# A fused two-block transformer step on Trainium2: the delta rule's inverse by six doubling levels of 64-column products, the gate's silu in two gaps, and a shorter router shift

## The reference, cut to what matters

```python
def gated_delta_rule(q, k, v, g, beta):          # 4 heads, chunks of the sequence
    ...
    a_low = jnp.where(strict, einsum('bnhie,bnhje->bnhij', kb, kc) * decay, 0.0)
    lhs = a_low + jnp.eye(C)
    u = triangular_solve(lhs, vb, left_side=True, lower=True)
    w = triangular_solve(lhs, kb * exp(gc)[..., None], left_side=True, lower=True)
    ...                                          # then the scan over chunks: state, outputs
# in hybrid_mixer
    o = rms_norm(o, dn_norm_w) * silu(dz)        # the gate's silu
    return concatenate([attn_out, dn_out], -1) @ w_out
# in routed_moe, with h = norm(x) * (1 + scale2) + shift2
    logits = xt @ w_router + b_router
```

## Time and profile before

| | |
|---|---|
| median of 3 runs | 2151.72 us (2151.05 to 2152.26) |
| the profiled execution | 2151.87 us, its span 2150.0 us |
| mean granted TensorE clock | 0.994 |
| PE busy | 2079.7 us (97%) |
| PE weight load | 1149.2 us (53%) |
| DVE busy | 978.7 us (46%) |
| ACT busy | 327.8 us (15%) |
| POOL busy | 50.3 us (2%) |
| chain that ended last | PE 80%, DMA 12%, DVE 4% |
| HBM | 590.91 MB read, 276 GB/s over the span |

### The profile page before, as it was taken

The page is one execution under the profiler, slowest core; times in us unless marked ns, Lnnn a source line. Parts: engine busy times, 40 slices in busy tenths (PEclk is TensorE's granted clock), DMA queues, the critical chain, the costliest instruction groups (busy, mean ns, idle before and its releaser), DMA issues.

```text
span 2150.0 us, 24181 instructions
## 1 busy us (share of the span) xinstructions
PE 2079.7 (97%) x9736; PEld 1149.2 (53%) x9736; DVE 978.7 (46%) x1573; ACT 327.8 (15%) x730; POOL 50.3 (2%) x30
## 2 busy tenths in 40 slices
PE   5999999999999999999999899999999999999999
PEld 3858533333333333333233456878884648868874
DVE  1486443333333333333322255734676167626684
ACT  1142100000010000000000113311110113311110
POOL 0001000000000000000000002000000011000000
PEclk9999999999999999999999999999999999999999
DMA  9548199999999999999999735324442634244441
GB/s 372 215 190 359 61 383 414 428 428 428 428 428 426 427 428 428 427 427 428 428 427 427 290 136 179 139 85 158 149 157 98 223 119 158 103 132 150 149 157 53
DMA packets 132917, 593.53 MB, mean 276 GB/s; under 512 B 9247, under 2 KB 65743, under 8 KB 104651
## 3 DMA queue, kind: packets, MB, share of 16 engines
q1 hardware_dynamic: 132810, 592.01, 69.4%
HBM read 590.91 MB, written 3.18 MB: 276 GB/s over the span
## 4 chain that ended last, share of the span: by engine, by line
PE 80%; DMA 12%; DVE 4%; issue 1%; ACT 1%; POOL 0%; SPq 0%; POOLq 0%; DVEq 0%
PE bank L1620 23%; PE bank L676 21%; DMA ring<-in_w_dram 11%; PE bank L686 8%; PE bank L2749 6%; PE bank L2712 3%; PE bank L1761 2%; PE bank L2727 2%; PE bank L1601 2%; PE bank L955 2%; PE bank L3103 1%; PE bank L1637 1%; DMA ring<-in_w_ada_dram 1%; DVE arena L1285 1%; PE bank L590 1%
## 5 line engine op out<-in xcount | busy, mean ns | idle before, releaser
L1620 PE MATMUL bank<-ring,arena 128*64 128x512 f32 x2304 | 509.8, 594 | 12.6 <-DMA ring<-in_w_dram 11.1
L676 PE MATMUL bank<-wide,ring 128*128 128x256 f32 x2368 | 517.2, 381 | 2.8 <-ACT wide L2980 2.6
L676 PEld LDWEIGHTS bank<-wide,ring 128*128 128x128 f32 x2368 | 451.0, 191 | 67.5 <-issue 5.9
L1620 PEld LDWEIGHTS bank<-ring,arena 128*64 128x64 f32 x2304 | 161.0, 137 | 351.3 <-issue 321.5
L1261 DVE TENSOR_SCALAR arena<-bank 128x512 f32<-128x512 f32 x32 | 22.1, 692 | 377.2 <-PE bank L1620 377.2
L686 PE MATMUL bank<-ring,wide 128*128 128x512 f32 (+2 forms) x384 | 151.4, 554 | 0.0
L2409 DVE SCALAR_TENSOR_TENSOR arena<-bank,arena 128x254 f32<-128x254 f32 (+1 forms) x176 | 76.6, 476 | 84.7 <-ACT arena L2553 83.2
L686 PEld LDWEIGHTS bank<-ring,wide 128*128 128x128 f32 x384 | 72.6, 190 | 74.6 <-issue 71.3
L1265 DVE RECIPROCAL arena<-arena 128x512 f32<-128x512 f32 x32 | 107.3, 3353 | 1.1
L1437 ACT ACTIVATE arena<-arena 128x512 f32<-128x512 f32 x32 | 20.1, 629 | 493.9 <-DVE arena L1261 493.9
L1620 PE MATMUL bank<-wide,arena 128*64 128x512 f32 x392 | 89.0, 595 | 0.7 <-ACT arena L1441 0.7
(11 more groups left out here) (515 smaller groups left out, 1961.4 us busy)
## 6 DMA issues: line engine op xcount, KB each, us to landing
ring<-in_w_dram SPq DMA_DIRECT2D x144, 2048.0 KB, 25.7
wide<-in_w_dram SPq DMA_DIRECT2D x24, 2048.0 KB, 26.3
arena<-in_w_dram SPq DMA_DIRECT2D x22, 2048.0 KB, 28.4
ring<-in_w_up_dram SPq DMA_DIRECT2D x44, 1024.0 KB, 6.8
ring<-in_w_in_dram SPq DMA_DIRECT2D x21, 2048.0 KB, 8.3
ring<-in_w_ada_dram SPq DMA_DIRECT2D x12, 2048.0 KB, 9.2
ring<-in_w_down_dram SPq DMA_DIRECT2D x10, 2048.0 KB, 7.8
ring<-in_w_out_dram SPq DMA_DIRECT2D x6, 2048.0 KB, 9.3
```

What stands on the lines that cost most here:

```text
L676: ins = pe.matmul(B.bank(name, j)[:, i * T:(i + 1) * T], w[:, k, (first + i) * P:(first + i + 1) * P], hT[:, k, :], start=(k == 0), stop=( ...
L1620: ins = pe.matmul(bank[g * SLOTS:(g + 1) * SLOTS, :], lhsT, rhs[:, g * CH:(g + 1) * CH], start=start, stop=stop)
```

## The change

The squares (`p2`, `p4`, `zz`, `xx`) go. The inverse starts from blocks of 2 (the identity minus the pairs' lower elements, masks `pair` and `pairT`) and doubles in six levels, 2 to 128. In a level a product takes only the columns that change: every second group of columns of the right operand, 64 of 128, so a job is four products of 64 columns (still eight instructions) into half a bank, its copy and its update handle half the elements. `T1` gets a zeroed place per level (GpSimd memsets), `BT` two places. The scaled operands are made before the levels. The silu of the gate moves to two places earlier in VectorE's stream, and its exponentials on ScalarE with it. shift2 comes as columns by a DMA of its own in `spread(sp, 1)`; the router's shift is a row (one weight column), `brow` of one partition, and a product with ones broadcasts it. On SP, the ten small parameter loads move to behind `dno`, ahead of `b12`; `norm_mix` and `final_norm_w` move behind the last expert chunk, and with them the wait for `h_new`. The constants' table has three masks for the last levels and a second load for the other five.

```diff
@@ first_plan
-                    ("p2", 4), ("p4", 2), ("zz", 4), ("xx", 4)):
-    for lv in range(4):
+    for lv in range(LEVELS):                     # LEVELS = 6
         p.add(f"bx{lv}", 2)
-        p.add(f"xl{lv}", 4 if lv < 3 else 2)
-    for name, n in (("shc", 1), ("br", 1), ("u0", 1), ("u1", 1), ("wT", 1), ("st", 1), ...
+        p.add(f"xl{lv}", 4 if lv < LEVELS - 1 else 2)
+    for name, n in (("u0", 1), ("u1", 1), ("wT", 1), ("br", 1), ("st", 1), ("ws", 1), ("qs", 1), ("brb", 1), ...
@@ spread(sp, g)
+            if g == 1:
+                sp.dma_start(split(shc, 4), mod_rows[0, 2:4, :].rearrange("i (c p k) -> p (i c) k", c=2, k=2))\
+                  .then_inc(S["mod_in1"], 16)
@@ helpers
+        t1_at = [biasbuf[:, D:2 * D], area(13312, D), area(13312 + D, D), area(0, D), normw[0][:]]
+        def level(m, lv, odd):
+            L = 2 << lv
+            return m.rearrange("p (b two r) -> p b two r", two=2, r=L)[:, :, odd, :]
@@ delta_pool
+            pool.memset(t1_at[0], 0.0).then_inc(S["t1z"], 1)
+            for due in B.all_taken(("t1", 4)):
+                pool.wait_ge(*due)
+            pool.memset(area(13312, 2 * D), 0.0).then_inc(S["t1z"], 1)
+            pool.wait_ge(*B.ready("o1"))
+            pool.memset(t1_at[3], 0.0).then_inc(S["t1z"], 1)
+            for lv in range(LEVELS):
+                ...                              # level 0: waits for kq and aT; two more memsets at level 2
+                if lv > 1:
+                    pool.wait_ge(*B.ready(f"bx{lv - 2}", 1))
+                pool.tensor_tensor(BT[lv % 2], AT, everywhere(c(f"low{lv}"), 8), ALU.mult).then_inc(S["bmat"], 1)
@@ silu, called behind scaled_v and between the two result_v
+        z_exp = [hbuf[:, 0:DW], normw[0][:, DW:2 * DW]]
+        def z_silu_v(v, then, tt):
+            v.wait_ge(S["zx"], tt + 1)
+            e = z_exp[tt]
+            then(v.tensor_scalar(e, e, 1.0, None, ALU.add))
+            then(v.reciprocal(e, e))
+            ins = v.tensor_tensor(dz[:, tt, :], dz[:, tt, :], e, ALU.mult)
+            ins.then_inc(S["zdone"], 1)
+            v.wait_ge(S["zdone"], tt + 1)
@@ delta_v
             ...                                  # Am, XTm: masked with pairT, pair, plus the identity; e_mat 1 to 4
-            for tt in range(TT):                 # the silu of both halves
-            ...
             v.wait_ge(S["gexp"], 1)
             ...                                  # bg, Vt, KBG, Kdec: now here, ahead of the levels
+            for lv in range(LEVELS):
+                for n, j in enumerate(XJOBS if lv < LEVELS - 1 else XJOBS[1::2]):
+                    m = tile_level((Am, XTm)[j // 2], j % 2, lv, j // 2)
+                    if lv:
+                        v.wait_ge(*B.taken(f"xl{lv - 1}", n if lv < LEVELS - 1 else 2 * n + 1))
+                    v.wait_ge(*B.ready(f"xl{lv}", n))
+                    v.tensor_tensor(m, m, narrow(half4(f"xl{lv}", n), lv), ALU.subtract).then_inc(B.free(f"xl{lv}", n), 1)
-            v.tensor_tensor(brow, B.bank("br")[:, 0:NE], brt, ALU.add).then_inc(B.free("br"), 1)
+            v.tensor_tensor(brow[0:1, :], B.bank("br")[0:1, 0:NE], brt[0:1, :], ALU.add).then_inc(B.free("br"), 1)
             ...
+            v.wait_ge(*B.ready("brb"))
+            v.tensor_copy(brow, B.bank("brb")[:, 0:NE]).then_inc(B.free("brb"), 1)
@@ delta_s
-            for nm, dst in (("p2", (P2, P2T)), ("p4", (P4,))):
-            ...
+            for lv in range(LEVELS):
+                act.wait_ge(S["t1z"], (1, 2, 2, 3, 4, 5)[lv])
+                for j in range(2):
+                    act.wait_ge(*B.ready(f"bx{lv}", j))
+                    act.activation(tile_level(T1[lv], j, lv, 0), narrow(half4(f"bx{lv}", j), lv), ACT.Copy)\
+                       .then_inc(B.free(f"bx{lv}", j), 1)
@@ delta_t
-            pe.wait_ge(S["e_mat"], 2)
-            ...                                  # p2, p4, zz, xx, four levels
+            pe.wait_ge(S["e_mat"], 4)
+            def half_product(lhsT, rhs, lv, odd):
+                return lambda out, u: pe.matmul(out.rearrange("p (b r) -> p b r", r=2 << lv), lhsT[:, u, :],
+                                                level(rhs[:, u, :], lv, odd), start=True, stop=True)
+            for lv in range(LEVELS):
+                t1, last = T1[lv], lv == LEVELS - 1
+                pe.wait_ge(S["bmat"], lv + 1)
+                for tt in range(2):
+                    if lv:
+                        pe.wait_ge(*B.taken(f"xl{lv - 1}", 2 * tt))
+                    half(f"bx{lv}", tt, half_product(BT[lv % 2], Am, lv, 0), tt)
+                for tt in range(2):
+                    pe.wait_ge(*B.taken(f"bx{lv}", tt))
+                    if lv:
+                        pe.wait_ge(*B.taken(f"xl{lv - 1}", 2 * tt + 1))
+                    if not last:
+                        half(f"xl{lv}", 2 * tt, half_product(XTm, t1, lv, 0), tt)
+                    half(f"xl{lv}", tt if last else 2 * tt + 1, half_product(t1, XTm, lv, 1), tt)
+            ...
-            ...                                  # shc, br ahead of u0
             four("u0", 0, product(XTm, Vt), 0)
             four("u1", 0, product(XTm, Vt), 1)
             four("wT", 0, product(KBG, XTm), 1)
+            for k in range(KT):
+                ins = pe.matmul(B.bank("br")[0:1, 0:NE], shc[:, k:k + 1], wrt[:, k, :], start=(k == 0), stop=(k == KT - 1))
+            ...
+            pe.matmul(B.bank("brb")[:, 0:NE], c("ones")[0:1, 0:P], brow[0:1, :], start=True, stop=True)\
+              .then_inc(B.full("brb"), 1)        # behind qs, ahead of od
@@ scalar: exponentials of the gate
+            act.wait_ge(*B.taken("z", 0))
+            act.activation(z_exp[0], dz[:, 0, :], ACT.Exp, scale=-1.0).then_inc(S["zx"], 1)
             ada_rows_s(act, 1)
             turned_s(act, B, jobs1[0], 0, PT)
             decays_s(act)
-            for j in range(TT): ...              # both exponentials were here
+            act.wait_ge(*B.taken("z", 1))
+            act.activation(z_exp[1], dz[:, 1, :], ACT.Exp, scale=-1.0).then_inc(S["zx"], 1)
@@ SP, behind dno and in later_sync
                     sp.wait_ge(S["dno"], 1)
+                    layer_params(sp, 0, late=False)
                     ...                          # b12
-            layer_params(sp, 0, late=False)
-            sp.wait_ge(S["h_new"], 4)
-            layer_params(sp, 0, early=False)
             for m in range(DEEP, NCH):
                 ...
-                if m == 2 * DEEP + DEEP - 1:
-                    sp.dma_start(normw[0][:], A["final_norm_w"].partition_broadcast(P)).then_inc(S["norm_in"], 16)
                 ...
+            sp.dma_start(normw[0][:], A["final_norm_w"].partition_broadcast(P)).then_inc(S["norm_in"], 16)
+            sp.wait_ge(S["h_new"], 4)
+            layer_params(sp, 0, early=False)
```

More of the change, by code:

```diff
@@ L137, in constants @@
     parts["early"] = -BIG * (f < p)
[L138 to L141, removed]
+    masks = {}
+    for lv in range(-1, LEVELS):
+        L = 2 << lv if lv >= 0 else 1
+        masks[f"low{lv}"] = (p // (2 * L) == f // (2 * L)) & ((f // L) % 2 == 1) & ((p // L) % 2 == 0)
+    for lv in range(3, LEVELS):
+        parts[f"low{lv}"] = masks[f"low{lv}"]
     for qt in range(TT):
@@ L169, in constants @@
     parts["bucket"] = (np.arange(P)[:, None] == bucket[None, :])
+    parts["pair"], parts["pairT"] = masks["low-1"], masks["low-1"].T
+    for lv in range(3):
+        parts[f"low{lv}"] = masks[f"low{lv}"]
     where, at, cols = {}, 0, []
@@ L697, in build_program @@
         XTm = units(area(10 * D, D))
-        P2, P2T, P4 = units(area(6 * D, D)), units(biasbuf[:, 0:D]), units(biasbuf[:, D:2 * D])
-        BT, T1, KBG = units(biasbuf[:, 0:D]), units(biasbuf[:, D:2 * D]), units(biasbuf[:, 2 * D:3 * D])
-        Kdec = split(area(6 * D, CH), 4)
+        BT = [units(area(9 * D, D)), units(area(6 * D, D))]
+        t1_at = [biasbuf[:, D:2 * D], area(13312, D), area(13312 + D, D), area(0, D), normw[0][:]]
+        T1 = [units(t1_at[lv % 5]) for lv in range(LEVELS)]
+        KBG = units(biasbuf[:, 2 * D:3 * D])
+        Kdec = split(biasbuf[:, CH:D], 4)
         Vnew = units(area(9 * D, D))
@@ L823, in delta_v @@
[L823 to L830, removed]
+            v.tensor_tensor(XTm, XTm, everywhere(ident, 8), ALU.add).then_inc(S["e_mat"], 1)
@@ L990, in delta_t @@
-            updates("zz", XJOBS, P2, None)
-            updates("xx", XJOBS, P4, "zz")
-            for lv in range(4):
-                last = f"xl{lv - 1}" if lv else "xx"
-                pe.wait_ge(S["bmat"], lv + 1)
-                for j in range(2):
-                    for i in range(2):
-                        pe.wait_ge(*B.taken(last, 2 * j + i))
-                    four(f"bx{lv}", j, product(BT, Am), j)
-                jobs = XJOBS if lv < 3 else XJOBS[1::2]
-                for n, j in enumerate(jobs):
-                    if n % (len(jobs) // 2) == 0:
-                        pe.wait_ge(*B.taken(f"bx{lv}", j % 2))
```

(27 more changed lines are left out.)

101 lines of the change are left out of this document (46 added, 55 removed), and 1 row of the table p.

## The result

The kernel after took 2169.61 us (median of 4 runs, 2168.42 to 2170.62) against 2151.99 us of the kernel before, timed beside it: a ratio of 1.0077 (95% interval [1.0064, 1.009]). It is slower by 17.6 us (16.6 by the ratio), where 12 less was forecast. Its profiled execution has a span of 2167.1 us (before 2150.0) and a mean granted clock of 0.983 (0.994).

What follows compares the result with a forecast made beforehand. TensorE bounds up to about 884 us, then the experts' DMA stream, whose start follows TensorE, then TensorE again. 10.8 us on TensorE plus 1.2 of loads, 12.0 off 2151.87, and 0.15 for the median, gave 2139.7 us; range 2135 to 2145.

Steps and rivals of the forecast that it cites:

- The clock: u0, u1 and wT behind the levels: TensorE back at 2.4 GHz, 2.68 us instead of 4.28, 1.60 less.
- rival 1: Half-width products lower TensorE's clock inside the levels: +31 us with all 34 jobs slow, about 2171 us; chance 0.09.
- The start: Ahead of level 0: VectorE's preparations done at 179.4 us, before TensorE is free at 181.6; 0 to 1.5 us allowed.
- The products: Delta rule's levels: 34 jobs of 64 columns for 36 of 128, each still 0.893 us.
- Rival 2: 64-column products cost half, so hand-overs bound a level at about 2.8 us: 13 us more gain, about 2126; chance 0.05.
- What a level waits for: No wait inside a level, so the levels take 30.4 us; 0.84 us of waiting stays behind the last update.
- The silu in two gaps: The gate's silu, 4.55 us each, fits VectorE's idle 4.63 and 5.51 us; cost 0 to 0.3, taken as 0.
- Rival 4: Clock still dips behind the idle 0.84 us before u0: 1.6 to 4.1 us more, 2141 to 2144; 0.75 together with the forecast.
- The router's shift: Ahead of u0, 5.91 us go; in their place 1.1 us of one-column products and 0.2 for the broadcast.
- The loads: final_norm_w leaves the experts' full stream, 1.2 us; backlog 0, at most 2; the moved small loads stay hidden.
- Rival 3: The experts' stream doesn't follow TensorE, as something else holds its chunks: half of 10.8 us lost, about 2145; chance 0.09.
- The sum: 10.8 us on TensorE's path plus 1.2 from the loads: 12.0 us less, -0.56%.

Runs made afterwards that it cites:

- narrow_gapless: Kernel after with GpSimd's second mask behind VectorE's four preparations and the scaled operands moved behind levels 1 and 2; 64-column products: 2138.24 us, 0.9942 of before.
- wide_gapless: narrow_gapless with the products of all six levels streaming 128 columns: 2139.18 us, 0.9943 of before.
- loads_back: narrow_gapless with SyncE's load order of before (parameters and h_new's wait ahead of chunk 8, final_norm_w at chunk 23): 2141.61 us, 0.9947 of before.
- before_router: Kernel before with the change's new router shift alone: 2152.65 us, 0.9998 of before.
- back_wide4: narrow_gap3 with level 4 alone streaming 128 columns: 2149.34 us, 0.9983 of before.
- narrow_prompt: Kernel after with GpSimd's second mask made only behind VectorE's four preparations, products still 64 columns: 2166.55 us, 1.0059 of before.
- narrow_gap3: narrow_gapless with GpSimd's level 3 mask held until level 2's last product, so TensorE waits 2.54 us ahead of level 3: 2156.51 us, 1.0021 of before.
- silu_back: narrow_gapless with both silus behind the fourth preparation, ahead of level 0's updates, and ScalarE's exponentials in their old place: 2169.49 us, 1.0074 of before.
- wide_gap3: wide_gapless with GpSimd's level 3 mask held until level 2's last product is done: 2143.29 us, 0.9959 of before.
- mixed_prompt: Kernel after with GpSimd's second mask behind the four preparations and 128-column products in levels 0 and 3 only: 2143.94 us, 0.9976 of before.

## Why the prediction was wrong, step by step

- *The clock* (rival 1) is the step that failed: the sum took all 34 jobs at 1.00, 30.4 us, and they took 56.25 at 0.50. "The 64-column products of L625 left it at 1.00" was true and no evidence: they ran while it was up. Rival 1 had the price and the time right: 0.213 us an instruction measured for 0.226, 25.9 us for 31, 2169.6 for 2171. Its mechanism was half right: in these runs 64 columns didn't lower the clock, but kept it low. I gave it 0.09 because I weighed the width alone and not what a wait would do to it.
- *The start* failed with it, and set it off. I priced VectorE's four preparations and GpSimd's masks each as if alone: 4 x 1.2 us, done at 179.4. Two of them ran beside the masks, 3.4 us each, and the four took 9.0 us, done at 182.1. "I allow 0 to 1.5" counted a wait as its own length; here each microsecond of it stood for more than ten. The Trainium skill ("SBUF — State Buffer", Who interferes with whom) says that a VectorE instruction with two inputs in SBUF and a GpSimd instruction that reads SBUF exclude each other. The durations of after agree: 3.39 is 1.21 plus most of a mask's 2.37, and the mask that began behind L851 grew as well. I had not weighed it.
- *The products* held at full clock: 0.112 us an instruction at 64 columns, 30.52 us for the 34 jobs of narrow_gapless (forecast 30.4). Rival 2 is out: wide_gapless and narrow_gapless are within 1 us. (The terms it lists for a level add up to 2.55 us, not to 2.8.)
- *What a level waits for* held: 5.36 us a level in narrow_gapless, 0.63 us ahead of u0 (forecast 0.84).
- *The silu in two gaps* held. VectorE's timeline in after, both gaps behind the silus still open:

```profile
155.40 0.17 DVE L804 COPY small<-bank 128x8 f32<-128x8 f32 x1 [0.57 <-PE bank L976]
...
167.08 0.69 DVE L563 TENSOR_TENSOR arena<-bank,small 128x512 f32<-128x512 f32 x1 [0.94 <-PE bank L637]
```

- *Rival 4* is not gone with the old shift: loads_back's profile has u0 at half clock behind 0.63 us of idling, 1.6 us more. narrow_gapless's has not.
- *The router's shift*: br 0.56 us for the forecast 1.1, brb 0.33 for 0.2. But the credit of 5.91 us belongs to two edits; alone it gave nothing (before_router), because I hadn't asked what ran beside the removed piece.
- *The loads*: the size fits (1.0 for 1.2), the parameters (259.30 to 263.6 us in after) delayed nothing that was seen: the first sum, at 271.33, still waited for TensorE, by 0.45 us. Rival 3 is out: chunk 8 moved by 16.5 us with TensorE's 17.2 in after, by 14.15 in narrow_gapless (285.53 to 271.38), where the transposes came 13.4 earlier.
- *The sum*: with the wait removed the kernel takes 2138.24 us, by the ratio 0.58% under before (0.68% by the medians), forecast 0.56%. The forecast was of a kernel without a wait ahead of its narrow products. In its profile 2.8 us of the 14.4 in span are an earlier start of the levels (178.8 for 181.6), in which the change has no part that I can show: in the profiles of the change's kernels the third modulation product ends at anything from 178.8 to 182.1. The other 11.6 are the sum (12.0).
- Shown is the clock's part in the loss (narrow against wide, with and without a wait, back_wide4). Not shown is why one wait starts a fall and another of its length doesn't.

The Trainium skill ("TensorE: Matmul & The Clock Gate", HAM oscillation — how this bites in real kernels) tells of a kernel in which each group of matmuls is shorter than the wait for a DMA behind it, and the clock drops for every group. Here it was single waits, for other engines: after, narrow_prompt, narrow_gap3 and silu_back agree that a wait can bring a drop; the profiled runs of wide_gap3, with 2.54 us of waiting, and of mixed_prompt, with 1.90, show none.

## What to carry to other kernels

Before a stretch of narrow matmuls, count each possible wait of TensorE at the price of the low clock over the whole stretch, not at its own length; keep one stage of full-width products behind a wait that can't be avoided, where width costs nothing, as here: 0.112 us an instruction at 64 and at 128 columns. Price two-input VectorE work beside GpSimd work at the sum of both. Before crediting a removed piece, list what the other engines did beside it.

## What the hardware showed that I had not expected

- At 0.50 of the clock, 64-column products with 128x128 weights held it there for over 50 us of unbroken work (after: 186 to 238.4); 128-column products at the same pace had it back within 3.2 us (back_wide4). Why the width decides this is not shown.
- At 1.00 both widths take 0.112 us an instruction, at 0.50 both 0.213.
- VectorE with two SBUF inputs beside GpSimd, both on 1024 floats a partition: 1.21 becomes 3.4 us, the mask 2.36 becomes 3.4. The one that was already running kept its time (L851 in after).
- 3.82 us of waiting made a kernel 31 us slower (silu_back against narrow_gapless).
